# A new order for the attention steps of a two-layer transformer trunk, on all engines

## The reference, cut to what matters

```python
x = LN(alpha*x + 0.5*swiglu_1(x))
x = LN(alpha*x + mixer(x))
x = LN(alpha*x + 0.5*swiglu_2(x))
```

## Time and profile before

| what | value |
| --- | --- |
| median of the timed runs | 1003.26 us |
| the profiled execution's own time | 1008.5 us |
| its span, first to last instruction | 1006.7 us |
| TensorE matmuls busy | 975.1 us, 97% |
| VectorE busy | 657.5 us, 65% |
| ScalarE busy | 508.2 us, 50% |
| mean granted TensorE clock | 0.992 of full speed |

### The profile page before, as it was taken

The page is one execution under the profiler, slowest core; times in us unless marked ns, Lnnn a source line. Parts: engine busy times, 40 slices in busy tenths (PEclk is TensorE's granted clock), DMA queues, the critical chain, the costliest instruction groups (busy, mean ns, idle before and its releaser), DMA issues.

```text
span 1006.7 us, 14735 instructions
## 1 busy us (share of the span) xinstructions
PE 975.1 (97%) x5288; PEld 823.3 (82%) x5288; DVE 657.5 (65%) x938; ACT 508.2 (50%) x680; POOL 10.3 (1%) x23
## 2 busy tenths in 40 slices
PE   6999999999989999999999999999999899999997
PEld 4988888878767888888888888887887679888885
DVE  3555555689887656555675565658888785565555
ACT  3554545445764555554455454554475644545451
POOL 0000000000000000000000000000000000000000
PEclk9999999999998999999999999999999999999999
DMA  8655657564323565656655555564742246555561
GB/s 285 210 191 184 201 179 238 186 210 168 126 84 125 168 208 167 208 167 214 204 173 202 179 197 185 190 234 155 251 168 85 72 138 209 182 194 187 194 203 42
DMA packets 123234, 180.25 MB, mean 179 GB/s; under 512 B 5696, under 2 KB 97984, under 8 KB 122432
## 3 DMA queue, kind: packets, MB, share of 16 engines
q1 hardware_dynamic: 122912, 178.45, 53.5%
q0 software_dynamic: 288, 1.34, 0.4%
HBM read 178.72 MB, written 1.05 MB: 179 GB/s over the span
## 4 chain that ended last, share of the span: by engine, by line
PE 91%; DVE 4%; ACT 2%; issue 1%; DMA 1%; SPq 0%; DVEq 0%
PE bank L507 26%; PE bank L509 14%; PE ybank L458 9%; PE ybank L464 9%; PE ybank L462 9%; PE bank L430 3%; PE bank L396 3%; PE bank L437 2%; PE bank L434 2%; PE ybank L430 2%; PE ybank L437 2%; PE ybank L434 2%; PE bank L491 2%; PE bank L487 2%; PE bank L493 2%
## 5 line engine op out<-in xcount | busy, mean ns | idle before, releaser
L1000 DVE TENSOR_TENSOR w_lo<-raw,w_hi 128x2048 fp32r<-128x2048 f32 (+1 forms) x162 | 371.0, 2290 | 245.7 <-ACT w_hi L788 245.7
L788 ACT ACTIVATE w_hi<-raw 128x2048 fp32r<-128x2048 f32 (+1 forms) x162 | 309.6, 1911 | 257.1 <-PE bank L509 112.1
L507 PE MATMUL bank<-xT,w_hi 128*128 128x512 f32 x1152 | 401.0, 392 | 0.0
L509 PE MATMUL bank<-xT,w_lo 128*128 128x256 f32 x1152 | 323.7, 281 | 0.0
L507 PEld LDWEIGHTS bank<-xT,w_hi 128*128 128x128 f32 x1152 | 216.2, 188 | 47.3
L509 PEld LDWEIGHTS bank<-xT,w_lo 128*128 128x128 f32 x1152 | 216.7, 188 | 1.5
L458 PE MATMUL ybank<-w_hi,yT_hi 128*128 128x512 f32 x416 | 166.8, 401 | 5.6 <-issue 2.9
L464 PE MATMUL ybank<-w_hi,yT_lo 128*128 128x512 f32 x416 | 163.6, 393 | 0.0
L462 PE MATMUL ybank<-w_lo,yT_hi 128*128 128x512 f32 x416 | 163.0, 392 | 0.0
L458 PEld LDWEIGHTS ybank<-w_hi,yT_hi 128*128 128x128 f32 x416 | 78.9, 190 | 24.7 <-issue 8.6
L464 PEld LDWEIGHTS ybank<-w_hi,yT_lo 128*128 128x128 f32 x416 | 78.4, 189 | 18.6
(11 more groups left out here) (119 smaller groups left out, 952.2 us busy)
## 6 DMA issues: line engine op xcount, KB each, us to landing
raw<-in_ffn_in SPq DMA_DIRECT2D x176, 512.0 KB, 4.6
raw<-in_ffn_out SPq DMA_DIRECT2D x88, 512.0 KB, 3.9
raw<-in_w_in SPq DMA_DIRECT2D x40, 512.0 KB, 4.5
raw<-in_w_o SPq DMA_DIRECT2D x16, 512.0 KB, 3.7
gb<-in_ln_gb SPq DMA_DIRECT2D x6, 1024.0 KB, 7.3
raw<-in_w_in SPq DMA_DIRECT2D x4, 520.0 KB, 6.4
out_dram<-xn SPq DMA_DIRECT2D x2, 512.0 KB, 2.6
cst<-in_consts POOLq DMA_DIRECT2D x1, 800.0 KB, 7.7
```

The source lines that it names most:

```text
L507: eng.matmul(dst[:, :], wh[:, k, g, cols], xT[:, kk, :, :].rearrange("p a n -> p (a n)"), start=kk == 0, stop=False, skip_group_check=True)
L509: m = eng.matmul(dst[:, SEQ:2 * SEQ], wl[:, k, g, cols], xT_hi[:, kk, :], start=False, stop=kk == KT - 1, skip_group_check=True)
L788: eng.activation(w_hi[:, s, 0:width], raw[:, s, 0:width], ACT.Copy).then_inc(hi_done, 1)
L1000: eng.tensor_tensor(w_lo[:, s, 0:width], raw[:, s, 0:width], w_hi[:, s, 0:width].bitcast(F32), ALU.subtract).then_inc(lo_done, 1)
```

## The change

It changes the order of the instructions of four engines' lists in the attention steps; which instructions there are stays the same.

- TensorE: parts of `FILL` move, so that step 0 has four parts behind the scores and steps 1 to 5 none there, but one behind each head's transposes. The transposes of head 0 so stand directly behind the scores. Step 4 gets a part between the transposes of head 1 and `values`; step 6 gets (12,1,0) between the transposes. The transposes of the convolution's accumulator no longer begin step 6; they stand behind the transposes of head 11, ahead of the last `values`.
- ScalarE: the order within a step was copy 0, exponent 0, copy 1, exponent 1; it is copy 0, exponent 0, exponent 1, copy 1. The two copies of step 3 to `fqT` and `fkT` stand behind that. `split_hi` moves ahead of the copy to `yT_hi` in steps 0 to 5; `begin_sum` of step 3 moves behind it.
- VectorE: one tap more in the projection part; the other 15 are in steps 0 (4), 2 (3), 4 (5), 5 (2) and 6 (1), and in up to four places of a step. The normalisation of the convolution is cut in two, with the last `y_split_lo` between.

```diff
-FILL = {0: ([(9, 0, 0), (9, 0, 1), (9, 1, 0)], [], [], []),
-        1: ([(9, 1, 1)], [], [(10, 0, 0)], []),
-        2: ([(10, 0, 1)], [(10, 1, 0)], [(10, 1, 1)], []),
+FILL = {0: ([(9, 0, 0), (9, 0, 1), (9, 1, 0), (9, 1, 1)], [], [], []),
+        1: ([], [(10, 0, 0)], [(10, 0, 1)], []),
+        2: ([], [(10, 1, 0)], [(10, 1, 1)], []),
         3: ([], [(11, 1, 0)], [(11, 1, 1)], []),
-        4: ([(11, 0, 0)], [(11, 0, 1)], [], []),
-        5: ([(12, 0, 0)], [(12, 0, 1)], [(12, 1, 0)], []),
-        6: ([], [], [], [(12, 1, 1)]),
+        4: ([], [(11, 0, 0)], [(11, 0, 1)], []),
+        5: ([], [(12, 0, 0)], [(12, 0, 1)], []),
+        6: ([], [(12, 1, 0)], [], [(12, 1, 1)]),
...
+STEP_TAPS = {0: (0, 1, 2, 1), 2: (0, 1, 1, 1), 4: (2, 1, 1, 1), 5: (1, 0, 1, 0), 6: (1, 0, 0, 0)}
-for _where, _n in [(("unit", 4), 3), (("unit", 6), 3), (("unit", 8), 5), (("unit", 9), 3)] + \
-        [(("step", s), n) for s, n in enumerate((3, 1, 4, 1, 4, 3))]:
+for _where, _n in [(("unit", 4), 3), (("unit", 6), 3), (("unit", 8), 5), (("unit", 9), 4)] + \
+        [(("step", s, i), n) for s, ns in STEP_TAPS.items() for i, n in enumerate(ns)]:
...
+            def conv_out_T(l):
+                eng.wait_ge(mx_ready, count(mx_ready, l, HEADS))
+                eng.wait_ge(conv_step, count(conv_step, l, CB * CONV_K))
+                transposes(bank[0], [acc[:, cb, t * P:(t + 1) * P] for t in range(T) for cb in range(CB)])\
+                    .then_inc(convT_psum, 1)
...
-                    if s < len(SLOTS):
+                    if s < CONV_SLOT:
                         scores(l, s)
...
                         if lagged and i in (1, 2):
                             probs_T(l, SLOTS[s - 1][1], i - 1)
+                        if s == CONV_SLOT and i == 3:
+                            conv_out_T(l)
                         if lagged and i == 3:
                             values(l, SLOTS[s - 1][1])
...
-                    for i in range(2):
-                        if lagged:
-                            probs_out(SLOTS[s - 1][1], i)
-                        if kind == "pair":
-                            exponent(p, i)
...
+                    if lagged:
+                        probs_out(SLOTS[s - 1][1], 0)
+                    if kind == "pair":
+                        exponent(p, 0)
+                        exponent(p, 1)
+                    if lagged:
+                        probs_out(SLOTS[s - 1][1], 1)
+                    for i in range(2 if s == FQ_STEP else 0):
...
-                    if s in BEGIN_AT:
+                    if s in BEGIN_AT and s != FQ_STEP:
                         begin_sum(l, 1, BEGIN_AT[s])
+                    if s in HI_AT and s < CONV_SLOT:
+                        split_hi(l, b, HI_AT[s])
                     if lagged:
...
                         eng.activation(yT_hi[:, Y_KT[pair], :], bank[3][:, 0:SEQ], ACT.Copy).then_inc(y_hi_done, 1)
+                    if s in BEGIN_AT and s == FQ_STEP:
+                        begin_sum(l, 1, BEGIN_AT[s])
...
-                    y_split_lo(l, s)
+                    step_taps = [TAPS_AT.get(("step", s, i), ()) for i in range(4)]
+                    if s <= CONV_SLOT:
+                        y_split_lo(l, s)
+                    taps(l, step_taps[0])
                     if kind == "pair":
                         mask_and_max(l, 2 * p)
                         mask_and_max(l, 2 * p + 1)
-                    if s == CONV_SLOT:
-                        conv_norm_first(l)
                     if s - 1 in HI_AT and s < CONV_SLOT:
                         split_lo(l, b, HI_AT[s - 1])
-                    step_taps = TAPS_AT.get(("step", s), ())
+                    taps(l, step_taps[1])
                     if kind == "pair":
                         inverse(l, 2 * p)
                         normalise(l, 2 * p)
-                        taps(l, step_taps[:1])
+                        taps(l, step_taps[2])
                         inverse(l, 2 * p + 1)
                         normalise(l, 2 * p + 1)
-                        taps(l, step_taps[1:])
+                        taps(l, step_taps[3])
+                    if s == CONV_SLOT:
+                        conv_norm_first(l)
+                        y_split_lo(l, s + 1)
+                        conv_norm_second(l)
```

More of the change, by code:

```diff
@@ L583, in scores @@
                     eng.wait_ge(mx_ready, count(mx_ready, l, 2 * SLOTS[s - 1][1] + 2))
[L584 to L589, removed]
                 fox = p >= DIL_H // 2
@@ L953, in mixer @@
                     lagged = s > 0 and SLOTS[s - 1][0] == "pair"
-                    for i in range(2):
-                        if lagged:
-                            probs_out(SLOTS[s - 1][1], i)
-                        if kind == "pair":
-                            exponent(p, i)
[L959 to L963, removed]
-                    if s in BEGIN_AT:
+                    if lagged:
[6 more added lines that the diff above has]
+                    for i in range(2 if s == FQ_STEP else 0):
+                        eng.wait_ge(proj_done, count(proj_done, l, 5 * T + i + 1))
+                        eng.activation((fqT, fkT)[i][:, :, :], ybank[i][:, :].rearrange("p (k n) -> p k n", k=2),
+                                       ACT.Copy, scale=(-HD ** -0.5, 1.0)[i]).then_inc(qkT_ready, 1)
+                    if s in BEGIN_AT and s != FQ_STEP:
                         begin_sum(l, 1, BEGIN_AT[s])
+                    if s in HI_AT and s < CONV_SLOT:
+                        split_hi(l, b, HI_AT[s])
                     if lagged:
@@ L978, in mixer @@
                            .then_inc(yaT_hi_done, 1)
-                    if s in HI_AT:
-                        split_hi(l, b, HI_AT[s])
                 split_hi(l, b, 16)
@@ L1164, in conv_norm_first, with conv_norm_second @@
                                              ALU.subtract, ALU.mult).then_inc(cln_step, 1)
+            def conv_norm_second(l):
                 for t in range(T):
```

## The result

The changed kernel took 989.54 us in the median (988.68 to 990.16) against 1003.15 us in the same comparison, ratio 0.9845 with a 95% interval of 0.9823 to 0.9867. In a second comparison, with 23 executions of the kernel before, it took 989.39 against 1006.46: 0.9836 (0.9812 to 0.9861). The changed kernel's medians agree and those of the kernel before differ by 3 us.

What follows compares the result with a forecast made beforehand. TensorE's instruction list plus its holes was taken as the bound (matmuls cover 97% of the span). Removing 20.0 us and leaving 2.2 gains 17.8: 1003.3 - 17.8 = 985.5 us, range 982.5 to 992, chance 0.62.

Steps and rivals of the forecast that it cites:

- It stands 5.2 us above the median of the runs, which I carry over: Whole kernel: profiled execution's 5.2 us excess over the median also holds after the change, so 990.7 becomes 985.5 us.
- The waits: TensorE's holes in both layers' attention steps: 20.0 us removed including 3.8 of clock, 2.2 left.
- The clock: Half-clock stretches at the end of step 6 in both layers go: 3.8 us of the 20.0.
- Transposes directly behind scores, filling behind each: Steps 1 to 6: filling removes 0.91, 0.91 and 0.82 us a layer; earlier transposes cost 0, in step 6 up to 0.5.
- Exponents side by side, split ahead of the copy: ScalarE's attention steps: paired exponents cost 0, or 0.2 us a step if they slip; earlier split lets y's copy start about on time.
- Unit 11: 0.4 left: Filling unit 11, waiting for y of pair 1: wait falls from 1.73 to 0.4 us a layer.
- Taps: VectorE before the accumulator's transposes: 35.0 us of work in 38.5; 0.4 us wait remains, plus 0.1 at values, per layer.
- The tail: 0.2: After the accumulator's transposes: unit 13 waits 0.2 us a layer for the last y's remainder, behind the normalisation's first half.
- The second: VectorE bounds the attention steps, last tap's wait 2 us longer in each layer: 989.5 us, chance 0.17.
- The third: Waits go but the clock still falls after the light end of step 6: 989.3 us, chance 0.12.
- The fourth: Feed-forward block takes the time back because its weights don't come sooner: 1003 us, chance 0.03.
- the fifth: Split ahead of y's copy stalls ScalarE on late loads, delaying four engines: 1013.7 us at 5 us late, chance 0.03.

Runs made afterwards that it cites:

- the undisturbed one: The kernel before, with no edit, profiled again in an execution at a granted clock of 0.999: 1003.48 us.
- the experiment: The changed kernel with only ScalarE's order put back to the old one: 991.99 us.

## Why the prediction was right or wrong

The time, 989.5 us, lies in the range, and the direction was right. The most likely value, 985.5, was 4.0 us too low. One step failed, and it is not in the attention steps.

- *"It stands 5.2 us above the median of the runs, which I carry over"*. That took the 5.2 us for something the changed kernel's profiled execution would have too. They were the clock's falls in that one execution: by the stretch, 64.10 - 61.40 = 2.70 in layer 0 and 62.86 - 61.39 = 1.47 in layer 1, and 0.9 more at the very start (its first scores come at 255.97 instead of 255.06, PEclk of the first 20 us 0.91 instead of 1.00). The sum counted 3.8 of them as gain, and then took them off a median whose executions did not have them. The profile even offered the check: three timed runs within 1.5 us of each other, and the profiled one 4 us above the highest. How large the error looks is partly luck: none of the first comparison's four executions took over 1004.6 us, but 38 of the later 52 did. With the later median of 1006.46 in the same sum the forecast would have been 988.7.
- *The waits.* Removed 20.0 - 3.8 = 16.2 us, left 2.2, net 14.0. Measured between executions at full clock: 2 x (61.4 - 54.4) = 13.9 by the stretch, 13.7 by time. From 1003.1 that gives 989.1. The sign "each part 8.5 to 9.5 us shorter" was for the profile with the falls: 9.66 and 8.42 against it, 6.96 and 6.95 against the undisturbed one.
- *The clock.* 3.8 us forecast for the profiled execution, 4.2 found. Of the gain against the typical execution, 17.1 us, some 3.4 are the clock's. The forecast of 17.8 is near that and wrong against the first comparison's four executions. The prediction also places the fall too late. It names the stretch from 297.63 to 304.77 as what went before; in layer 0 the clock fell at 301.7, behind the hole of 1.71 us and during the next, and the last hole and the values of pair 5 were already at 1.2 GHz.
- *Transposes directly behind scores, filling behind each.* Right and the core of it: without it the other two lists bring no time, and with only the place of one part in each of five steps altered 6.63 of 6.96 us are lost. VectorE did have `prob` ready in each step.
- *Exponents side by side, split ahead of the copy.* Forecast at no cost; the experiment puts the gain of ScalarE's whole order at 1.36 us a layer, 1.04 of it at head 11, where the place of the split decides, and most of the rest at the scores of pair 4, where the exponents' does. The sum counted this among the waits removed, without a line of its own.
- *Unit 11: 0.4 left.* 0.27. The copy to `yT_hi` began at 272.91 right behind the split, with values at 271.66.
- *Taps.* 0.4 at the last one and 0.1 at values: 0.23 and 0.12 (294.30 - 293.82 - 0.25, and 294.89 - 294.30 - 0.47). The budget of 35.0 us of work in 38.5 us held, VectorE being busy 35.49 of 38.74. With VectorE's old list, the taps' old places and the undivided normalisation together, 2.59 us a layer come back; no run separates the two.
- *The tail: 0.2.* Under 0.1: the two products around 297.34 follow each other with 0.38 instead of some 0.3.
- *The rivals.* The second, VectorE as the bound: the time it gave, 989.5, came, but not its cause. No wait of over 0.3 us for the last tap is in the trace, so this agreement proves nothing. The third, the clock falling still, gave 989.3, as near and as wrong: the clock is 1.00 at that place in both profiles of the changed kernel; the fall came with less filling. The fourth and the fifth: from one attention part to the next it takes as long as before (739.15 - 309.52 = 429.6 after, 746.20 - 316.46 = 429.7 in the undisturbed execution), and no copy of y came more than 0.3 us late behind a split.

The changed kernel has transposes directly behind scores in five places of a layer, and its lowest clock was 0.996. The Trainium skill says that transposes do not count as busy for the clock in the way other matmuls do ("TensorE: Matmul & The Clock Gate", Part 4: PE-mode transpose). That brought no fall in the attention steps of the changed kernel's two profiles. A fall does not need transposes either: in layer 1 of the kernel with only TensorE's list old it came inside a hole. Whether they helped it along where they stood between the holes, no run here tells.

What stays open is what decides in each execution whether the clock falls, and where it fell in the changed kernel's executions at 0.996 and 0.997, none of which was profiled. What is left of waits in the attention steps is some 0.7 us a layer, too little for a further order to be told by time, so none was tried.

## What to carry to other kernels

Between two uses of a single buffer, put independent work that is longer than the copy that frees it, and look at which side of the pair it stands: with the same filling one place earlier 6.63 of the 6.96 us were lost. An order spread over three engines has to be judged together: TensorE's alone brought 3.8 us a layer, those of ScalarE and VectorE 3.2 on top of it. Alone these two removed 1.5 us of waits in layer 0 but lengthened the hole at the last tap from 1.71 to 2.19 us, and the clock took the time back. Where waits are left, their place matters as well as their sum. Before the profiled execution's time is scaled to the median, compare its mean clock with that of the timed executions: a slow stretch in the profile that the timed runs in the median don't have is no gain to be counted against them, and a constant offset is a claim to be checked.

## What the runs showed of the hardware that was not expected

One program on one core has several times: 13 of 52 executions at a granted clock of 0.999 and 1003.1 us, 37 at 0.995 or less and 1004.8 to 1008.7 us. The clock fell from 2.4 to 1.2 GHz in the attention steps although TensorE had not idled longer than 1.71 us at a time there. In layer 0 it had, from 297.63 to the fall at 301.7, nothing besides values, transposes, that hole and the greater part of the next one of 0.67; in layer 1 it fell only toward the end of the third hole, the 0.58. In the earlier trace rows the stretch 289.00 to 300.20, up to the end of the hole of 1.71, has 2.5 us of holes and filling ahead of them, and the clock held through it. With a hole of 2.19 us in its place the clock was 0.994 or less in 12 of 12 executions; with the holes spread between filling it was 0.996 or more in 12 of 12.

The clock also falls near the start of the span, and there the ten profiles sort by the first long hole: 3.05 us (the kernel before) and 2.90 (only TensorE's list old) in the two that fell, 2.21 to 2.57 in the eight that did not. Both times it fell over 1 us after TensorE had begun again, at 14.9 us behind the restart at 13.74, and at 15.1 behind 13.81, amid products of 512 columns.

The Trainium skill ("TensorE: Matmul & The Clock Gate", Part 1) says of the clock's rise at the start of a kernel that its place varies from run to run. Here it is the fall in the middle of a kernel that varies so, with up to 6.5 us between executions of one program.
